# Cross-attention in a two-block fp32 kernel: scores ahead of the value projection, softmax and transposes beside it, output results in pairs

## The chip, the core and the metric

One core of a Trainium2 chip runs the whole program. The metric is the device time of one execution in microseconds; the kernel before took 3685.83 us (median of three runs).

## The reference, cut to what matters

Two transformer-like blocks run one after the other over 256 tokens of width 1024. The first has two layers (l = 0, 1), each a feed-forward network, a mixer, the cross-attention that is changed here, and a second feed-forward network:

```python
def memory_cross_attention(h_n, mem_n, wq, wkv, wo):     # 4 heads of 256
    q = (h_n @ wq).reshape(bsz, seqlen, XA_HEADS, XA_HEAD_DIM)
    mk, mv = jnp.split(mem_n @ wkv, 2, axis=-1)
    ...
    s = jnp.einsum('bshd,bmhd->bhsm', q, mk).astype(jnp.float32) * (XA_HEAD_DIM ** -0.5)
    pr = jax.nn.softmax(s, axis=-1).astype(mv.dtype)
    o = jnp.einsum('bhsm,bmhd->bshd', pr, mv).reshape(bsz, seqlen, D_MODEL)
    return o @ wo

for l in range(DEPTH):                                    # DEPTH = 2
    ...
    h = h + y @ w_mix_out[l]
    h = h + memory_cross_attention(rmsnorm(h, xattn_norm[l]), rmsnorm(mem, mem_norm[l]), xattn_wq[l], xattn_wkv[l], xattn_wo[l])
    h = h + FFN_RES * swiglu_ffn(rmsnorm(h, ffn2_norm[l]), ffn2_w_in[l], ffn2_w_out[l])
```

Everything is fp32. A second block (attention, experts) follows and is the same in both kernels.

## The kernel before, in words

**Weights.** All weights come as one stream of 128x128 blocks, packed into chunks of 32 blocks (2 MB). The SyncE queue loads chunk c into one of three ring slots as soon as the chunk three places earlier is released by TensorE. A product with a weight is made of three fp32r products (`mm3`): high by high, high by low, low by high. So each chunk has to be split before TensorE can use it: a cast into one of two "high" buffers and a subtraction that leaves the low half in the ring slot. In this part of the program VectorE does both (`dve_split`, L389 and L390), and it may not start before TensorE has released the chunk two places earlier, whose high buffer it takes. `act_cast` and `dve_lows` are the same job shared between ScalarE (cast) and VectorE (subtraction). Most products have 96 matmuls of 256 columns to a chunk; those of the value projection have 48 of 512 columns.

**Order.** Each engine's program is a list written in Python order, and an engine runs its list strictly in order. Waits are on counters: `mark(name)` lets an instruction count when it is done, `at(name)` is the value to wait for. VectorE and ScalarE also wait for their own previous instruction. `take` gives out the eight PSUM banks in turn and waits until the bank's last result has been read (`left`).

**Cross-attention of one layer.** Call its first chunk c0. TensorE does, in this order: query projection `xq` (chunks c0, c0+1, eight results of 24 matmuls, with the two norm sums after the first); key projection `xk` (c0+2, c0+3); value projection `xv` (c0+4, c0+5, two halves `n` of two banks each); the attention proper, `pe_attention`; output projection `xout` (c0+6, c0+7). Then the second feed-forward network begins with chunk c0+8: 48 matmuls for its first result, the norm sum, and on. The attention has eight jobs (head h, half of the queries qt). A job is a score product (2 fp32 matmuls), maximum (VectorE), exponential (ScalarE), normalising (VectorE), two transposes on TensorE (`turn`), a copy (ScalarE), the value product (4 fp32 matmuls) and two copies out (VectorE). `Attention.run` staggers them: round i issues the scores of job i+1, the transposes of job i-2 and the values of job i-3. After all eight jobs VectorE makes the high and low halves of the attended values one 128x256 block after the other (L1780, L1781), and `xout` starts when the first is ready.

VectorE's list around this: the split of c0+1; two reciprocals; the normed memory in eight steps of three instructions (L1762, L1764, L1765); four query results; the split of c0+2; four query results; the split of c0+3; and from there each split stands just ahead of the results of the chunk before it. At the end, `xout` result m is added to the stream X (L1785) and two instructions (L525, L526) make the halves that the feed-forward network's products take in the order k = m.

Of the kernel before, what the change touches and what calls it, by code (L numbers as in the profile page):

```python
# [10 lines left out]
ALU = mybir.AluOpType  # L11
# [227 lines left out]
def build(nc, x_t, mem_t, ctx_t, params, consts, na_bias, wexp, xd, yd, out):  # L239
    es = ExitStack()  # L240
    with es:
# [32 lines left out]
        for i, o in enumerate((4096, 5120, 10240, 11264, 17664, 18688, 19712, 20736)):  # L274
            out_parts.append(nc.alloc_sbuf_tensor_at(f"arena_out{i}", [128, 1024], F32R, offset=arena_at + 4 * o))
        psb = [es.enter_context(nc.psum_tensor(f"ps{i}", [128, 512], F32)) for i in range(8)]
# [1427 lines left out]
        XQ, XK, XO, XV = Reg(12288, 2048), Reg(14336, 2048), Reg(16384, 2048), Reg(18432, 2048)  # L1704
        RM = mrow[:, 256:512]

# [3 lines left out]
        def attended_halves(l):  # L1710
            return Halves(("xo", l), lambda k: XO.v(256 * k, 256), lambda k: MN.v(256 * k, 256), as_r)

        def cross(l):
            jobs = []
            for h in range(4):
                for qt in range(2):
                    jobs.append(([XQ.v(256 * (2 * h + j) + 128 * qt, 128) for j in range(2)],
                                 [XK.v(256 * (2 * h + j), 256) for j in range(2)],
                                 [XV.v(1024 * b + 256 * h, 256) for b in range(2)], 256, None,
                                 [XO.v(256 * (2 * h + m) + 128 * qt, 128) for m in range(2)]))  # L1720
            return Attention(("cross", l), jobs, 1.0 / 16, [Reg(20480, 512).v(), Reg(20992, 512).v()],
                             [Reg(21504, 512).v(), Reg(22016, 512).v()],
                             [("left", ("xq", l), 7), ("left", ("xk", l), 6), ("left", ("xk", l), 7), ("left", "xv", l, 1, 1)])

        def pe_xattn(pe, l):
            s = ("xattn", l)
            mh = memory_halves(l)
# [9 lines left out]

            pe_linear(pe, ("xq", l), ("xattn_wq", l), 0, 0, normed(s), range(KT), after=norms)
# [8 lines left out]
            pe_attention(pe, cross(l))  # L1747
            pe_linear(pe, ("xout", l), ("xattn_wo", l), 0, 0, attended_halves(l), range(KT))
            pe.here("pe", "xattn", l)

        def dve_xattn(dve, l):
            s, nxt = ("xattn", l), ("ffn2", l)
            mh, oh = memory_halves(l), attended_halves(l)
            for m in range(KT):
                dve_weights(dve, KT)
                if m == 0:
                    dve_norm(dve, s)
                    dve.wait_ge(*at("mem root", l))
                    dve.next.reciprocal(RM, RM).then_inc(*dve.mark("left", "mem norm", l))
                    for k in range(KT):  # L1760
                        hi, lo = mh.at(k)
                        dve.next.scalar_tensor_tensor(mh.lo(k), MEMr.v(256 * k, 256), par("mem_norm", l, k), RM, ALU.mult,  # L1762
                                                      ALU.mult).then_inc(*dve.mark())
                        dve.next.tensor_copy(hi, mh.lo(k)).then_inc(*dve.mark())  # L1764
                        dve.next.tensor_tensor(lo, mh.lo(k), hi.bitcast(F32), ALU.subtract).then_inc(*dve.mark("half", mh.name, k))  # L1765
# [7 lines left out]
            for n in range(2):  # L1773
                dve_weights(dve, 4 * KT)
                for b in range(2):
                    dve.wait_ge(*at("ps", "xv", l, n, b))
# [1556 lines left out]
```

## Time and profile before

| | |
|---|---|
| median of three runs | 3685.83 us (3681.63 to 3687.85) |
| profiled execution, its own time | 3680.79 us |
| its span in the trace | 3679.0 us |
| TensorE busy | 3409.8 us, 93% |
| VectorE busy | 2854.6 us, 78% |
| ScalarE busy | 1501.6 us, 41% |
| cross-attention, layer 0 and 1 (from the first query product) | about 513 to 642 us and 1350 to 1479 us |

The span is what the rows are measured in. A row of the timeline gives start and duration, then the instruction's group, and in square brackets how long the engine had been idle before it and who released it. TensorE's clock stands in the windows as a share of 2.4 GHz: 1.00 is 2.4 GHz and 0.50 is 1.2 GHz.

### The profile page before, as it was taken

The numbers are of one execution on the slowest core, as the hardware profiler recorded it, in microseconds if no ns is written. First come the engines' busy times: TensorE is split into PE (matmuls) and PEld (weight loads), VectorE is DVE, ScalarE is ACT, GpSimd is POOL, SyncE is SP. The second block draws the span as 40 slices with busy tenths as digits, with TensorE's granted clock in tenths as the row PEclk, the third lists the DMA queues.
The fourth block names the chain that finished last, engine by engine and source line by source line (L and its number), as shares of the span: only waits on it lengthen the run. The fifth ranks groups of instructions, "written<-read, shape, count | busy, mean of one in ns | idle before, by whom it ended". The sixth has DMA issues, their size and how long they took to land.

```text
span 3679.0 us, 53164 instructions
## 1 busy us (share of the span) xinstructions
PE 3409.8 (93%) x21102; PEld 2869.8 (78%) x21102; DVE 2854.6 (78%) x3335; ACT 1501.6 (41%) x2046; POOL 707.4 (19%) x461
## 2 busy tenths in 40 slices
PE   8998999999996999998888999999799789999996
PEld 8996788999994788997555777777687667777775
DVE  8877677888876667876758888888674688888884
ACT  1013121100013121111323888888531358888883
POOL 0000130100000230100001334344101024344430
PEclk9998989999998999999999999999999999999998
DMA  6544243455544243552015999999752169999993
GB/s 238 191 166 190 103 161 118 181 184 184 184 165 183 92 149 123 187 184 92 24 46 187 366 382 374 366 371 376 285 220 103 73 219 346 348 358 344 347 348 134
DMA packets 119853, 799.39 MB, mean 217 GB/s; under 512 B 33824, under 2 KB 35872, under 8 KB 49440
## 3 DMA queue, kind: packets, MB, share of 16 engines
q1 hardware_dynamic: 78480, 735.14, 53.7%
q0 software_dynamic: 39024, 59.61, 4.6%
q8 instruction: 170, 2.79, 0.3%
q10 hardware_dynamic: 2080, 1.05, 0.1%
q14 instruction: 99, 0.81, 0.1%
HBM read 808.77 MB, written 71.83 MB: 239 GB/s over the span
## 4 chain that ended last, share of the span: by engine, by line
PE 54%; DVE 10%; ACT 2%; DMA 1%; issue 1%; POOL 0%; DVEq 0%; SPq 0%; ACTq 0%; POOLq 0%
PE ps L443 50%; PE ps L457 4%; DMA ring<-yd_dram 1%; DVE ring_r L390 1%; DVE ring_r L2650 1%; DVE arena L2094 1%; DVE ring_r L389 0%; ACT arena L1699 0%; DVE mrow L1880 0%; ACT arena_hi L2714 0%; DVE arena_r L2664 0%; DVE arena_r L526 0%; DVE ring L2463 0%; DMA yd_dram<-arena,small 0%; DVE arena L2424 0%
## 5 line engine op out<-in xcount | busy, mean ns | idle before, releaser
L443 PE MATMUL ps<-arena_r,ring_r 128*128 128x256 f32 (+1 forms) x9968 | 1298.1, 290 | 48.5 <-DVE ring_r L390 20.9
L443 PEld LDWEIGHTS ps<-arena_r,ring_r 128*128 128x128 f32 x9968 | 1242.2, 191 | 88.9 <-DVE ring_r L390 21.5
L443 PE MATMUL ps<-ring_r,arena_r 128*128 128x512 f32 (+1 forms) x2906 | 800.5, 391 | 5.5 <-DVE arena_r L1966 5.1
L443 PEld LDWEIGHTS ps<-ring_r,arena_r 128*128 128x128 f32 x2906 | 530.6, 189 | 118.5 <-DVE arena_r L1966 5.5
L443 PE MATMUL ps<-arena_hi,arena_r 128*128 128x512 f32 x1540 | 507.3, 397 | 4.7 <-DVE ring_r L2675 4.7
L390 DVE TENSOR_TENSOR ring_r<-ring,ring_r 128x4096 fp32r<-128x4096 f32 (+2 forms) x108 | 469.5, 4347 | 3.7
L2791 POOL DMA_INDIRECT yd_dram<-arena,small x129 | 227.3, 1762 | 734.2 <-PE ps L457 640.3
L443 PEld LDWEIGHTS ps<-arena_hi,arena_r 128*128 128x128 f32 x1540 | 289.9, 188 | 68.8 <-DVE ring_r L2675 5.1
L389 DVE CAST ring_r<-ring 128x4096 fp32r<-128x4096 f32 (+2 forms) x108 | 268.9, 2490 | 65.0 <-PE ps L443 53.4
L2650 DVE TENSOR_TENSOR ring_r<-ring,ring_r 128x2048 fp32r<-128x2048 f32 x130 | 298.0, 2292 | 22.8 <-ACT ring_r L2714 15.7
L2650 DVE TENSOR_TENSOR ring_r<-ring,arena_hi 128x2048 fp32r<-128x2048 f32 x128 | 293.5, 2293 | 24.2 <-ACT arena_hi L2714 16.8
L2783 POOL DMA_INDIRECT arena<-xd_dram,small x129 | 267.7, 2076 | 150.1 <-DVE arena L2473 60.8
L443 PE MATMUL ps<-ring,arena 128*128 128x512 f32 (+1 forms) x708 | 271.6, 513 | 0.0
L443 PE MATMUL ps<-arena 64*128 64x128 f32 (+5 forms) x1472 | 216.4, 329 | 52.3 <-ACT arena L1699 25.2
L2714 ACT CAST ring_r<-ring 128x2048 fp32r<-128x2048 f32 x130 | 248.8, 1914 | 29.6 <-PE ps L443 18.2
L457 PEld LDWEIGHTS ps<-consts_sb,arena 128*128 128x128 f32 (+1 forms) x1532 | 173.7, 142 | 107.1 <-DVE arena L2669 77.4
L2714 ACT CAST arena_hi<-ring 128x2048 fp32r<-128x2048 f32 x128 | 244.4, 1910 | 11.4 <-ACT arena_hi L2714 0.4
L443 PEld LDWEIGHTS ps<-arena 128*128 128x128 f32 (+1 forms) x1472 | 164.4, 208 | 99.8 <-ACT arena L1699 51.4
L457 PE MATMUL ps<-consts_sb,arena 128*128 128x128 f32 (+1 forms) x1532 | 202.0, 276 | 26.7 <-DVE arena L1175 5.6
L2746 ACT COPY arena<-ps 128x512 f32<-128x512 f32 x258 | 151.2, 586 | 163.6 <-PE ps L443 150.9
L610 ACT ACTIVATE arena<-arena 128x256 f32<-128x256 f32 x88 | 36.8, 418 | 437.4 <-DVE arena L588 437.4
L2664 DVE TENSOR_TENSOR arena_r<-ps,arena_r 128x512 fp32r<-128x512 f32 x258 | 178.5, 692 | 31.1 <-ACT arena_r L2734 3.8
(328 smaller groups left out, 3459.5 us busy)
## 6 DMA issues: line engine op xcount, KB each, us to landing
ring<-wexp_dram SPq DMA_DIRECT2D x387, 1024.0 KB, 8.2
ring<-stream_dram SPq DMA_DIRECT2D x143, 2048.0 KB, 7.8
ring<-yd_dram SPq DMA_DIRECT2D x7, 2048.0 KB, 12.2
arena<-yd_dram SPq DMA_DIRECT2D x5, 2048.0 KB, 9.6
xd_dram<-arena POOLq DMA_DIRECT2D x6, 512.0 KB, 5.9
consts_sb<-consts_dram SPq DMA_DIRECT2D x1, 2242.0 KB, 16.1
arena<-xd_dram,small POOLq DMA_INDIRECT x129, 10.5
yd_dram<-arena,small POOLq DMA_INDIRECT x129, 8.8
```

The costliest lines, as they stand in the source:

```text
L389: dve.next.tensor_copy(chunk_hi(c, a, b), chunk_raw(c, a, b)).then_inc(*dve.mark())
L390: dve.next.tensor_tensor(chunk_lo(c, a, b), chunk_raw(c, a, b), chunk_hi(c, a, b).bitcast(F32), ALU.subtract).then_inc(*dve.mark())
L443: return pe.e.matmul(ps, lhsT=lhsT, rhs=rhs, start=start, stop=stop, skip_group_check=True)
L457: return pe.e.transpose(ps, src, ident[0:n, 0:n])
L610: act.next.activation(g[:, 0:256], g[:, 0:256], ACT.Silu, bias=0.0, scale=1.0).then_inc(*act.mark("silu", s, i))
L2094: dve.next.reciprocal(ARS.v(), ARS.v()).then_inc(*dve.mark("left", "ab norm", i))
L2650: dve.next.tensor_tensor(S.raw(part, i, rings_r), S.raw(part, i), S.hi(part, i).bitcast(F32), ALU.subtract).then_inc(*dve.mark(S.key, "spl ...
L2664: dve.next.tensor_tensor(lo, bank(K, "x", i, g)[:, :], hi.bitcast(F32), ALU.subtract).then_inc(*dve.mark("left", K, "x", i, g))
L2714: act.next.copy(S.hi(part, i), S.raw(part, i)).then_inc(*act.mark(S.key, "high", part, i))
L2746: act.next.copy(YB[i % 2].v(512 * nn, 512), bank(K, "y", i, nn)[:, :]).then_inc(*act.mark("left", K, "y", i, nn))
L2783: pool.e.indirect_dma_start(out=XB[i % 3].v(), out_offset=None, in_=xd, in_offset=bass.IndirectOffsetOnAxis(ap=TOKEN_OF[:, S.b0 + i:S.b0 + ...
L2791: pool.e.indirect_dma_start(out=yd, out_offset=bass.IndirectOffsetOnAxis(ap=PAIR_OF[:, S.b0 + i:S.b0 + i + 1], axis=0), in_=YB[i % 2].v(), ...
```

## The change

In both layers:
- The eight score products come right after `xk`, one in each PSUM bank, before `xv`. VectorE does all eight softmaxes there, ahead of the split of c0+5; the probabilities (`XP`) and their transposes (`XPT`) have a buffer for each job.
- The transposes of job i stand behind step i+3 of the 16 steps of `xv`, the value products of jobs 0 to 3 behind steps 12 to 15. Banks 0 to 3 serve `xv` and `xout`, banks 4 to 7 transposes and values (`take_of`).
- `xout` adds its results up two to a bank ("xout pair"), so that all eight can be open at once: first the products with k = 0, 1 for all m, then the value products of jobs 4 to 7, then k = 2, 3, then m by m k = 4 to 7.
- The attended values' high halves are copied from PSUM by ScalarE (`xo high`) and the low halves made from PSUM by VectorE (`low`), without the copies in between.
- The normed memory's cast goes to ScalarE. The casts of chunks c0+2 and c0+8 go to ScalarE (in quarters), VectorE keeps the subtractions: for c0+2 between the query results 3 and 4, for c0+8 ahead of the `xout` results. The high half of c0+8 has a home of its own (`ffn_parts`).

```diff
+        XP, XPT, XOH = Reg(20480, 2048), Reg(4096, 2048), XK
...
         def pe_xattn(pe, l):
+            cross_at[l] = pe.w.pos // CH
+            hi_home[cross_at[l] + 8] = ffn_parts
+            groups = {0: 0, 4: 0}
+
+            def take_of(first, *name):
+                pe.banks, pe.taken = range(first, first + 4), groups[first]
+                groups[first] += 1
+                return take(pe, *name)
...
+            def turn(i):
+                ps = take_of(4, "xt", l, i)
...
+            def values(i):
+                h = i // 2
+                ps = take_of(4, "xo", l, i)
...
             pe_linear(pe, ("xk", l), ("xattn_wkv", l), 0, 0, mh, range(KT))
+            pe.banks, pe.taken = range(8), 0
+            for i in JOBS:
+                scores(i)
             for n in range(2):
-                pss = [take(pe, "xv", l, n, b) for b in range(2)]
+                pss = [take_of(0, "xv", l, n, b) for b in range(2)]
...
+                    step = KT * n + k
+                    if 3 <= step < 11:
+                        turn(step - 3)
+                    if step >= 12:
+                        values(step - 12)
...
-            pe_attention(pe, cross(l))
-            pe_linear(pe, ("xout", l), ("xattn_wo", l), 0, 0, attended_halves(l), range(KT))
+            out_blocks([(m, k) for k in (0, 1) for m in range(KT)])
+            for i in range(4, 8):
+                values(i)
+            out_blocks([(m, k) for k in (2, 3) for m in range(KT)])
+            out_blocks([(m, k) for m in range(KT) for k in range(4, KT)])
...
         def dve_xattn(dve, l):
+            def normalise(i):
+                mx, sm, nm = softmax_cols(i)
+                dve.wait_ge(*at("left", "xs", l, i))
+                dve.next.reciprocal(sm, sm).then_inc(*dve.mark())
+                dve.next.tensor_scalar(XP.v(256 * i, 256), XP.v(256 * i, 256), sm, None, ALU.mult).then_inc(*dve.mark("xp", l, i))
...
             for m in range(KT):
+                if m == KT // 2:
+                    dve_lows(dve, c0 + 2, ((0, n_),), 1024)
                 dve_weights(dve, KT)
...
-            for n in range(2):
-                dve_weights(dve, 4 * KT)
...
-            dve_attention(dve, cross(l))
-            for k in range(KT):
-                dve.next.tensor_copy(oh.at(k)[0], oh.lo(k)).then_inc(*dve.mark())
...
+            for i in range(10):
+                if i < 8:
+                    largest(i)
+                if i >= 2:
+                    normalise(i - 2)
+            dve_weights(dve, 4 * KT)
+            values_out(0)
+            dve_weights(dve, 4 * KT)
+            for i in range(4):
+                low(i)
+            values_out(1)
+            dve_weights(dve, 4 * KT)
+            for i in range(4, 8):
+                low(i)
+            dve_lows(dve, c0 + 8, QUARTERS, 1024)
+            dve_weights(dve, 4 * KT)
             for m in range(KT):
-                dve_weights(dve, KT)
-                dve.wait_ge(*at("ps", ("xout", l), m))
...
+                dve.wait_ge(*at("ps", "xout pair", l, m // 2))
...
         def act_xattn(act, l):
+            for k in range(KT):
+                act.wait_ge(*at("mem normed", l, k))
+                act.next.copy(mh.at(k)[0], mh.lo(k)).then_inc(*act.mark("mem high", l, k))
+            act_cast(act, c0 + 2, QUARTERS, "released", c0)
...
-            act_attention(act, cross(l))
+            for i in JOBS:
...
+                              v3(bank("xo", l, i)[:, 0:256], 128)).then_inc(*act.mark("xo high", l, i))
+            act_cast(act, c0 + 8, QUARTERS, "ps", "xv", l, 1, 1)
```

On TensorE, before, the end of `xv` (banks 3 and 4) and the start of the attention (`arena`, fp32; L457 is a transpose) read:

```order
L443 MATMUL ps4<-ring_r_49,arena_r_50 128x512 x3
L443 MATMUL ps3<-ring_r_49,arena_r_50 128x512 x3
L443 MATMUL ps4<-ring_r_49,arena_r_50 128x512 x3
L443 MATMUL ps5<-arena 128x256 [waits dve_done,act_done]
L443 MATMUL ps5<-arena 128x256
L443 MATMUL ps6<-arena 128x256 x2
L443 MATMUL ps7<-arena 128x256 x2
L443 MATMUL ps0<-arena 128x256 x2
L457 MATMUL ps1<-consts_sb,arena 128x128 [waits dve_done]
L457 MATMUL ps1<-consts_sb,arena 128x128
L443 MATMUL ps2<-arena 128x256 x2
L443 MATMUL ps3<-arena 128x128 [waits act_done]
```

In the change (L445 is the same helper line), TensorE from the last key product (bank 0) to the start of `xv`:

```order
L445 MATMUL ps0<-arena_r_50,ring_r_49 128x256 x24
L445 MATMUL ps0<-arena 128x256 [waits dve_done,act_done]
L445 MATMUL ps0<-arena 128x256
L445 MATMUL ps1<-arena 128x256 x2
L445 MATMUL ps2<-arena 128x256 [waits dve_done]
L445 MATMUL ps2<-arena 128x256
L445 MATMUL ps3<-arena 128x256 x2
```

and its last steps of `xv` with the value products of jobs 2 and 3 (banks 6, 7), then the first `xout` pairs:

```order
L445 MATMUL ps2<-ring_r_49,arena_r_50 128x512 x3
L445 MATMUL ps3<-ring_r_49,arena_r_50 128x512 x3
L445 MATMUL ps6<-arena 128x128 [waits act_done]
L445 MATMUL ps6<-arena 128x128 x3
L445 MATMUL ps2<-ring_r_49,arena_r_50 128x512 x3
L445 MATMUL ps3<-ring_r_49,arena_r_50 128x512 x3
L445 MATMUL ps7<-arena 128x128 [waits act_done]
L445 MATMUL ps7<-arena 128x128 x3
L445 MATMUL ps0<-arena_r_50,ring_r_49 128x256 [waits dve_done]
L445 MATMUL ps0<-arena_r_50,ring_r_49 128x256 x5
```

The scores moved ahead of `xv` and wait for the last key result's copy, whose bank 0 is the first that they take; the value products moved between steps of `xv`, and `xout` follows without the eight-job block ahead of it.

On VectorE, before, from the last two key results to the end of `xv`'s results (`ring`: splits, L1777: value results), and then the first softmax:

```order
L1772 COPY arena<-ps 128x256 [waits dve_done,pe_done] x2
L389 CAST ring_r<-ring 128x4096 [waits dve_done,pe_done,chunk_loaded1]
L390 TENSOR_TENSOR ring_r<-ring,ring_r 128x4096 [waits dve_done]
L1777 COPY arena<-ps 128x512 [waits dve_done,pe_done] x2
L389 CAST ring_r<-ring 128x4096 [waits dve_done,chunk_loaded2]
L390 TENSOR_TENSOR ring_r<-ring,ring_r 128x4096 [waits dve_done]
L1777 COPY arena<-ps 128x512 [waits dve_done,pe_done] x2
L1657 TENSOR_REDUCE small<-ps 128x1 [waits pe_done]
```

In the change, the end of the eight softmaxes, then the splits of c0+5, c0+6 and c0+7 (L391, L392) among the value results (L1836) and the attended values (L1828):

```order
L1823 TENSOR_SCALAR arena<-arena,small 128x256 [waits dve_done]
L391 CAST ring_r<-ring 128x4096 [waits dve_done,chunk_loaded1]
L392 TENSOR_TENSOR ring_r<-ring,ring_r 128x4096 [waits dve_done]
L1836 COPY arena<-ps 128x512 [waits dve_done,pe_done] x2
L391 CAST ring_r<-ring 128x4096 [waits dve_done,chunk_loaded2]
L392 TENSOR_TENSOR ring_r<-ring,ring_r 128x4096 [waits dve_done]
L1828 TENSOR_TENSOR arena_r<-ps,arena_r 128x2x128 [waits dve_done,act_done] x4
L1836 COPY arena<-ps 128x512 [waits dve_done,pe_done] x2
L391 CAST ring_r<-ring 128x4096 [waits dve_done,pe_done,chunk_loaded0]
L392 TENSOR_TENSOR ring_r<-ring,ring_r 128x4096 [waits dve_done]
L1828 TENSOR_TENSOR arena_r<-ps,arena_r 128x2x128 [waits dve_done,act_done] x4
```

The split of c0+5 moved from directly behind the last key result to behind 32 softmax instructions.

## Rows read from the trace of the kernel before

**Rows 1.** Windows of layer 0, cut where TensorE's stages begin; busy us.
```profile
544.83:571.29 26.46, 23.94 (x192) 23.94 (x193) 19.31 (x13) 1.12 (x3) 0.00 (x0) 0.94 0.44 160
571.40:593.96 22.56, 22.56 (x98) 17.90 (x96) 15.48 (x7) 1.66 (x2) 0.00 (x0) 1.00 0.51 187
593.96:616.34 22.38, 17.52 (x114) 14.89 (x113) 14.36 (x53) 7.49 (x24) 0.00 (x0) 1.00 0.26 95
616.34:642.20 25.86, 25.45 (x193) 24.55 (x194) 24.28 (x32) 2.04 (x5) 0.00 (x0) 0.94 0.22 82
642.20:655.11 12.91, 11.10 (x65) 10.10 (x64) 10.99 (x12) 2.58 (x5) 0.00 (x0) 0.87 0.45 164
```

Columns of Rows 1: stretch and length, then busy time of TensorE's matmuls, its weight loads, VectorE, ScalarE and GpSimd (instructions), TensorE's clock, DMA share, GB/s.

**Rows 2.** Timeline, TensorE: queries into keys (layer 0), the same in layer 1, its end.
```profile
524.52 20.31 PE L443 MATMUL ps<-arena_r,ring_r 128*128 128x256 f32 x168
547.35 12.90 PE L443 MATMUL ps<-arena_r,ring_r 128*128 128x256 f32 x95 [2.52 <-DVE ring_r L390]
...
1384.45 24.12 PE L443 MATMUL ps<-arena_r,ring_r 128*128 128x256 f32 x192 [2.52 <-DVE ring_r L390]
...
1490.62 9.66 PE L443 MATMUL ps<-arena_r,ring_r 128*128 128x256 f32 x79
```

**Rows 3.** Timeline, ScalarE, layer 0: the copy of the last key result.
```profile
571.60 0.37 ACT L1796 COPY arena<-ps 128x256 f32<-128x256 f32 x1 [5.23 <-PE ps L443]
```

**Rows 4.** Timeline, TensorE inside the attention: scores with values, transposes, scores with values.
```profile
601.05 1.92 PE L443 MATMUL ps<-arena 128*128 128x256 f32 x12
602.81 0.38 PE L457 MATMUL ps<-consts_sb,mrow 128*128 128x128 f32 x2
603.03 2.07 PE L443 MATMUL ps<-arena 128*128 128x256 f32 x12
```

**Rows 5.** Timeline, TensorE, start of the second feed-forward network: products, norm sum, products.
```profile
645.64 0.62 PE L443 MATMUL ps<-arena_r,ring_r 128*128 128x256 f32 x3 [0.82 <-DVE arena_r L526]
647.07 4.94 PE L443 MATMUL ps<-arena_r,ring_r 128*128 128x256 f32 x27 [0.82 <-DVE arena_r L526]
651.85 3.62 PE L443 MATMUL ps<-arena,consts_sb 128*128 128x256 f32 x16
655.11 1.05 PE L443 MATMUL ps<-arena_r,ring_r 128*128 128x256 f32 x6
```

**Rows 6.** Timeline, VectorE: normed memory, query results, the split of c0+2.
```profile
527.89 0.48 DVE L1762 SCALAR_TENSOR_TENSOR arena<-arena,params_sb,mrow 128x256 f32<-128x256 f32 x1
528.41 0.29 DVE L1764 CAST arena_r<-arena 128x256 fp32r<-128x256 f32 x1
528.74 0.42 DVE L1765 TENSOR_TENSOR arena_r<-arena,arena_r 128x256 fp32r<-128x256 f32 x1
...
538.42 2.01 DVE L1767 TENSOR_TENSOR arena<-ps,mrow 128x256 f32<-128x256 f32 x4
540.54 2.29 DVE L389 CAST ring_r<-ring 128x4096 fp32r<-128x4096 f32 x1
542.87 4.43 DVE L390 TENSOR_TENSOR ring_r<-ring,ring_r 128x4096 fp32r<-128x4096 f32 x1
```

**Rows 7.** Timeline, ScalarE in the second block: a chunk cast in quarters.
```profile
2698.03 4.28 ACT L402 CAST ring_r<-ring 128x1024 fp32r<-128x1024 f32 x4
```

**Rows 8.** Timeline, VectorE: maximum and scaling of one job, normalising of another.
```profile
604.20 0.42 DVE L1657 TENSOR_REDUCE small<-ps 128x1 f32<-128x256 f32 x1
604.65 0.15 DVE L1658 TENSOR_SCALAR small<-small 128x1 f32<-128x1 f32 x1
...
605.85 0.16 DVE L1648 RECIPROCAL small<-small 128x1 f32<-128x1 f32 x1
606.05 0.35 DVE L1649 TENSOR_SCALAR arena<-arena,small 128x256 f32<-128x256 f32 x1
```

**Rows 9.** DMA issues, 500 to 660 us: KB each, median us to landing.
```profile
ring<-stream_dram SPq DMA_DIRECT2D x9, 2048.0 KB, 8.1
```

**Rows 10.** The page's costliest groups: transposes; busy us, mean ns of one, idle before.
```profile
L457 PE MATMUL ps<-consts_sb,arena 128*128 128x128 f32 (+1 forms) x1532 | 202.0, 276 | 26.7 <-DVE arena L1175 5.6
```

More of the change, by code:

```diff
@@ L275, in build @@
             out_parts.append(nc.alloc_sbuf_tensor_at(f"arena_out{i}", [128, 1024], F32R, offset=arena_at + 4 * o))
+        ffn_parts = [nc.alloc_sbuf_tensor_at(f"arena_ffn{i}", [128, 1024], F32R, offset=arena_at + 4 * o) for i, o in enumerate((8192, 9216))]
+        ffn_parts += out_parts[2:4]
         psb = [es.enter_context(nc.psum_tensor(f"ps{i}", [128, 512], F32)) for i in range(8)]
@@ L1710, in attended_halves, with attended, softmax_cols @@
         def attended_halves(l):
[L1711 to L1723, printed above, removed]
+            return Halves(("xo", l), lambda k: XO.v(256 * k, 256), lambda k: XOH.v(256 * k, 256), as_r)
+        def attended(reg, i):
+            return v3(reg[:, 512 * (i // 2):512 * (i // 2) + 512], 256)[:, :, col(i % 2)]
+        def softmax_cols(i):
+            return [small[:, 200 + 4 * i + j:201 + 4 * i + j] for j in range(3)]
         def pe_xattn(pe, l):
             s = ("xattn", l)
-            mh = memory_halves(l)
+            mh, oh = memory_halves(l), attended_halves(l)
+            cross_at[l] = pe.w.pos // CH
[5 more added lines that the diff above has]
+                return take(pe, *name)
             def norms(m):
@@ L1746, in pe_xattn, with out_blocks @@
                             *(("ps", "xv", l, n, b) if k == KT - 1 else ()), last=b == 1)
-            pe_attention(pe, cross(l))
-            pe_linear(pe, ("xout", l), ("xattn_wo", l), 0, 0, attended_halves(l), range(KT))
+                    step = KT * n + k
[3 more added lines that the diff above has]
+                        values(step - 12)
+            pairs = {}
+            def out_blocks(order):
+                for m, k in order:
+                    wb = blocks(pe, ("xattn_wo", l), 128 * k, 128 * m)
+                    if m % 2 == 0 and k == 0:
+                        pairs[m // 2] = take_of(0, "xout pair", l, m // 2)
+                    pe.wait_ge(*at("half", oh.name, k))
+                    mm3(pe, pairs[m // 2][:, col(m % 2, 256)], wb, oh.at(k), k == 0 and m % 2 == 0, k == KT - 1,
+                        *(("ps", "xout pair", l, m // 2) if k == KT - 1 and m % 2 else ()))
+            out_blocks([(m, k) for k in (0, 1) for m in range(KT)])
[3 more added lines that the diff above has]
+            out_blocks([(m, k) for m in range(KT) for k in range(4, KT)])
+            pe.banks = range(8)
             pe.here("pe", "xattn", l)
@@ L1796, in act_xattn @@
                 act.next.copy(XK.v(256 * m, 256), bank(("xk", l), m)[:, 0:256]).then_inc(*act.mark("left", ("xk", l), m))
-            act_attention(act, cross(l))
+            for i in JOBS:
+                mx, sm, nm = softmax_cols(i)
+                act.wait_ge(*at("xmax", l, i))
+                act.next.activation(XP.v(256 * i, 256), bank("xs", l, i)[:, 0:256], ACT.Exp, bias=nm, scale=1.0 / 16,
+                                    accum_out=sm).then_inc(*act.mark("left", "xs", l, i))
+            for i in JOBS:
+                act.wait_ge(*at("ps", "xt", l, i))
+                act.next.copy(XPT.v(256 * i, 256), bank("xt", l, i)[:, 0:256]).then_inc(*act.mark("left", "xt", l, i))
+            for i in JOBS:
+                act.wait_ge(*at("ps", "xo", l, i))
+                act.next.copy(attended(arena_r[:, XOH.base:XOH.base + 2048], i),
+                              v3(bank("xo", l, i)[:, 0:256], 128)).then_inc(*act.mark("xo high", l, i))
+            act_cast(act, c0 + 8, QUARTERS, "ps", "xv", l, 1, 1)
             for m in range(KT):
```

61 lines of the change are left out of this document (49 added, 12 removed).

## The prediction

> **What bounds the kernel now.** I read the page first (TensorE is busy for 93% of the span), then TensorE's timeline through the cross-attention of both layers, then windows cut where its stages begin, and last the timelines of VectorE and ScalarE for what releases it. TensorE's order is one long chain, so what counts is how much longer each stage takes than its products need.
>
> The needs first. A key result, 48 matmuls at two results, takes 0.37 + 5.23 = 5.60 us by the copies' rhythm [rows 3], so 192 matmuls take 22.4 us, and 48 take 5.6. The value projection takes 22.56 us with TensorE never idle [rows 1]. One score product and one value product together take 602.81 - 601.05 = 1.76 us, a job's two transposes 603.03 - 602.81 = 0.22 us [rows 4]; eight jobs need 14.1 + 1.8 = 15.9 us. The norm sum takes 655.11 - 651.85 = 3.26 us [rows 5]. From the end of the queries (544.83 us) to 655.11 us the products need 22.4 + 22.56 + 15.9 + 22.4 + 5.6 + 3.26 = 92.1 us.
>
> The stretch lasts 110.28 us, so 18.2 us are lost in layer 0, in four places [rows 1]:
> - Keys: 26.46 against 22.4, 4.1 lost. TensorE waits 2.52 us for the split of c0+2 [rows 2], and the window's mean clock is 0.94; the remaining 1.5 us is work done at half clock after the wait.
> - Attention: 22.38 against 15.9, 6.5 lost in round trips over VectorE and ScalarE.
> - Output: 25.86 against 22.4, 3.5 lost: `xout` begins while VectorE still makes halves, at a mean clock of 0.94.
> - Feed-forward start: 12.91 against 5.6 + 3.26, 4.0 lost: two waits of 0.82 us are shown for the last stream halves [rows 5], because results 4 to 7 stand behind a split, and the clock is 0.87 [rows 1].
>
> Layer 1 repeats this (the same 2.52 us wait, queries ending at 1384.45 - 2.52 = 1381.93) but is through at 1490.62 [rows 2]: 108.69 us, 16.6 lost. The clock does not drop at its end.
>
> **The change, part by part.** No product is added or removed on TensorE; the gain is the lost time less what is lost afresh. VectorE and ScalarE I walk through in their new order.
>
> Memory norm and c0+2. The memory's loop on VectorE starts at 527.89. A first product takes 0.52 us to the next start, a low 0.42 + 0.04; with the cast on ScalarE a step costs 0.98 instead of about 1.30, eight end at 536.2, four query results (2.01) at 538.2 [rows 6]. ScalarE has its last memory cast behind it at about 535.7 (the nearest row is a copy of 0.37 us, [rows 3]). It may then cast c0+2, since c0 is released after 72 of the 168 matmuls, at 524.52 + 72 x 0.121 = 533.2 [rows 2]. Four quarters take 4.28 us [rows 7]: 540.0. VectorE's subtraction takes 4.43 [rows 6]: 544.5. TensorE asks at 544.83. The 2.52 us wait goes, with 0.3 us to spare, and with it the half clock. If the casts come 2 us late, 1.7 us of wait returns, at worst with its 1.5 us of clock.
>
> What is late next: c0+3's split starts when four query results are out (546.6), takes 6.81 (540.54 to 547.35, [rows 2, 6]) and ends at 553.4; it is needed at 544.8 + 11.2 = 556.0.
>
> Scores and softmax. I now count from the end of the keys as t = 0. The first score takes bank 0, which holds the last key result, so it waits for ScalarE's copy: that starts 0.31 us after the keys end (571.29 to 571.60) and lasts 0.37 [rows 1, 3], with the signal 0.7 us. This is new idle time. Scores then run to 0.7 + 8 x 0.88 = 7.7 (0.88 is half of 1.76). On VectorE a job costs 0.42 + 0.15 + 0.16 + 0.35 [rows 8] and four gaps of 0.04, together 1.24 us; the first three maxima follow the scores (to 4.0), and the five maxima of 0.64 and eight normalisings of 0.60 left end at 12.0. Only then comes the split of c0+5, to 18.9. TensorE asks for it after half of the value projection and five jobs' transposes, at 7.7 + 11.3 + 1.1 = 20.1. It is hidden by 1.2 us; beyond that each microsecond costs one, and a wait like that of the keys brings its 1.5 us of clock.
>
> Value projection. It ends, with eight transposes and four value products (0.88), at 7.7 + 22.56 + 1.8 + 3.5 = 35.5. The split of c0+6 is ready at 20.1 + 1.5 + 6.9 = 28.5, the halves of jobs 0 and 1 well before. Behind it stand the halves of jobs 2 and 3, `xv` results and c0+7's split: 36.4 + 1.5 + 6.8 = 44.7, needed at 35.5 + 5.6 + 3.5 + 5.6 = 50.2.
>
> c0+8. Its slot is free at 34.7, a chunk lands 8.1 us after its issue [rows 9], 42.8. ScalarE reaches its casts after the last value copy, at 45.1, and ends at 49.4; VectorE's four quarters follow to about 50.5. The first `xout` pair is ready at 53.0, so nothing waits for it. A landing over 2.5 us later would hold the results behind the subtractions.
>
> Output. The last pair is ready at T = 50.2 + 11.2 = 61.4. VectorE handles one result in 647.07 - 645.64 = 1.43 us [rows 5], 2.86 a pair against 2.8 for TensorE to make one, so it has the last half ready at T + 3.1; TensorE asks for it at T + 7 x 0.35 = T + 2.45. Pairing costs 0.7 us here, in place of 4.0.
>
> Insertions. The transposes and values between `xv` steps bring 16 changes of product and wait per layer. The trace has none next to fp32r products of `xv`; in the attention the ends meet without a gap. Bounds: nothing, and one transpose slot of 0.11 us each, 1.8 us a layer. I take the middle, 0.9.
>
> Here the Trainium skill speaks against the move. Its page "TensorE: Matmul & The Clock Gate", section "Part 4: PE-mode transpose", gives about 275 ns to a transpose in a kernel. By that alone 16 transposes would take 4.4 us a layer. The profile's group agrees as a duration, 276 ns mean [rows 10], but durations overlap: two follow one another in 0.22 us [rows 4], so the sum above uses 0.11 each.
>
> **Sum.** Fresh losses are 0.7 + 0.7 + 0.9 = 2.3 us a layer. Layer 0 gains 18.2 - 2.3 = 15.9, layer 1 gains 16.6 - 2.3 = 14.3, together 30.2 us. I take 30: the span goes from 3679.0 to 3649, the profiled execution from 3680.8 to 3651. The median of before is 3685.83, 5 us above its profiled execution, and the forecast goes with the median: 3655.8 us. The feed-forward network behind runs on the same chunk rhythm, so the gain should reach the end.
>
> **The rivals.**
> - Transposes pay their full duration inside `xv`: 16 x 0.276 = 4.4 us instead of 1.8, 2.6 us more a layer. For: the 276 ns [rows 10]. Against: the spacing of 0.11 us [rows 4]. Gain 30 - 5.2, time 3661.
> - The softmax keeps its old pace. An old round lasted 603.03 - 601.05 = 1.98 us [rows 4]; eight at that pace from t = 1.7 end at 17.5, the split of c0+5 at 24.3, and TensorE waits 4.2 us plus 1.5 for the clock. For: VectorE needs the scores and ScalarE's exponentials between its steps. Against: the old pace was that of the round trip with TensorE, which is now gone. It costs 5.7 a layer: 3667.
> - c0+2 stays late, as the order on ScalarE has no slack of size: 3.2 us a layer, 3662.
> - The stream cannot deliver. The chunks are now used up in some 12 us each. Against: in the value projection the stream moved 187 GB/s while TensorE was never idle [rows 1], and a landing takes 8.1 us. If it did hold TensorE to the old mean, nothing would change: 3686.
> - Slower than before: the split of c0+5 behind 32 softmax instructions. The same mechanism as the second, from 3.2 us per job on: then the split ends at 33.7, TensorE waits 13.6 us and the clock takes 1.5, which eats the mean gain of a layer, 15.1. At 4 us a job the split ends at 40.5, the loss is 20.4 + 1.5 us a layer, and the time is 3699. Against: the rows add up to 1.24 us a job.
>
> **How the numbers follow.** The forecast with all splits hidden gets 0.72; transposes at full length 0.06, old softmax pace 0.08, c0+2 late 0.09, the stream 0.03, slower 0.02. The low end is all 34.8 us of lost time without any fresh loss, 3651, and 3 us for the spread between runs (3681.63 to 3687.85): 3648. The high end takes in the partial cases up to 3668. Within 0.2% (7.4 us) is what a measurement here cannot tell from no change. Faster 0.95, same 0.03, slower 0.02.
>
> **What would show it.** Right: the timeline of TensorE has no wait for a ring subtraction (L410, L392) at the start of the keys or in `xv`; windows through the whole cross-attention show clock 1.00; a wait of 0.7 us ahead of the scores and of about 0.7 for the last stream half; the stretch from the queries' end to the end of the feed-forward norm sum lasts 94 to 95 us in both layers. Wrong: a VectorE wait at c0+2 or in the middle of `xv`, a clock of 0.5 behind it, `xv` with its insertions far over 28 us, or a gain in the cross-attention that later stages give back.

## The result, and the profile after

The changed kernel took 3646.84 us (median of four, 3641.68 to 3652.22), the kernel before beside it 3683.73 us (3676.8 to 3687.85): a ratio of 0.99 with a 95% interval of 0.9887 to 0.9914. The forecast was 3655.8 us with a range of 3648 to 3668, so the result lies 1.2 us below the range. The profiled execution took 3648.08 us, its span 3646.3 us, 32.7 us less than before.

The windows of layer 0 after the change (columns as in [rows 1]; queries, keys, scores, value projection with its insertions, output projection, feed-forward start). One cut differs: [rows 1] cuts the keys at the end of the last query product, these windows at its start, 0.28 us earlier; the other cuts are alike.

```profile
521.94:541.80 19.86, 19.86 (x169) 19.83 (x168) 16.50 (x23) 7.94 (x13) 0.00 (x0) 1.00 0.29 107
541.80:564.60 22.80, 22.80 (x195) 22.68 (x193) 16.99 (x13) 1.12 (x3) 0.00 (x0) 1.00 0.51 185
564.60:572.16 7.56, 7.10 (x35) 6.09 (x34) 4.36 (x16) 4.45 (x12) 0.00 (x0) 1.00 0.77 277
572.16:600.21 28.05, 28.05 (x147) 23.11 (x145) 20.51 (x26) 5.83 (x18) 0.00 (x0) 1.00 0.21 76
600.21:626.95 26.74, 26.43 (x227) 26.20 (x226) 22.59 (x31) 8.59 (x15) 0.00 (x0) 1.00 0.43 158
626.95:636.48 9.53, 9.18 (x66) 8.59 (x65) 9.11 (x9) 2.12 (x3) 0.00 (x0) 1.00 0.60 222
```

The clock is 1.00 in every stage, where [rows 1] had 0.94, 0.94 and 0.87. The keys take 22.52 us (22.80 less the 0.28) instead of 26.46. The 22.38 us of the attention are gone: 7.56 us of scores stand alone, the value projection grew from 22.56 to 28.05 us by the transposes of eight jobs and the value products of four, and the value products of the other four are in the 26.74 us of the output stage. From the end of the last query product to behind the feed-forward norm sum it is 94.4 us in layer 0 (542.08 to 636.49) and 94.5 in layer 1; 94 to 95 was forecast.

The waits that are left, from TensorE's timeline after the change (layer 0, and the first of layer 1):

```profile
565.34 7.17 PE L445 MATMUL ps<-arena 128*128 128x256 f32 x32 [0.46 <-ACT arena L1897]
602.16 4.57 PE L445 MATMUL ps<-arena_r,ring_r 128*128 128x256 f32 x36 [0.31 <-DVE arena L1836]
629.94 0.51 PE L445 MATMUL ps<-arena_r,arena_ffn 128*128 128x256 f32 x2 [0.35 <-DVE arena_r L528]
...
1365.39 22.67 PE L445 MATMUL ps<-arena_r,ring_r 128*128 128x256 f32 x192 [0.45 <-DVE ring_r L410]
```

A bracket counts idle time from the end of the product before, and a product's row lasts 0.28 us where the next one can start 0.12 us behind it. So a wait costs about 0.2 us more than its bracket says.

The first is the wait for bank 0 and the copy of the last key result, the third the wait for the last stream half; both were forecast. The second was not: the third output pair takes bank 2, and the value projection's second half in it is read (L1836) only behind job 3's low half. The fourth is c0+2 in layer 1, whose 0.3 us of slack was a 0.45 us wait there. In layer 0 it had no slack either: the subtraction ends at 541.95 us and the first key product starts at 542.00, 0.08 us late, and 0.26 us late in the four other traces of the change.

VectorE after the change, around c0+5's split (L391, L392):

```profile
568.23 0.42 DVE L1816 TENSOR_REDUCE small<-ps 128x1 f32<-128x256 f32 x1 [0.25 <-PE ps L445]
569.61 0.43 DVE L1816 TENSOR_REDUCE small<-ps 128x1 f32<-128x256 f32 x1
570.98 0.42 DVE L1816 TENSOR_REDUCE small<-ps 128x1 f32<-128x256 f32 x1
577.96 2.29 DVE L391 CAST ring_r<-ring 128x4096 fp32r<-128x4096 f32 x1
580.29 4.43 DVE L392 TENSOR_TENSOR ring_r<-ring,ring_r 128x4096 fp32r<-128x4096 f32 x1
```

A softmax job takes 1.37 us, not 1.24, and the split ends at 584.72. TensorE's next rows show that it was just late:

```profile
582.80 0.38 PE L459 MATMUL ps<-consts_sb,arena 128*128 128x128 f32 x2
582.94 1.64 PE L445 MATMUL ps<-ring_r,arena_r 128*128 128x512 f32 x6
584.41 0.38 PE L459 MATMUL ps<-consts_sb,arena 128*128 128x128 f32 x2
584.77 1.66 PE L445 MATMUL ps<-ring_r,arena_r 128*128 128x512 f32 x6
```

Behind transposes the next product starts after 0.14 us, but here after 0.36: 0.2 us of wait, where 1.2 us of slack was forecast.

### The profile page after: what moved, and what is told of

Its sections match the earlier page's. It is cut to its first block, busy times and chain, and to the rows that moved or that the text cites. A ratio compares the mean times of both kernels' runs of the same rounds, so it can differ in the third digit from the quotient of the medians.

```text
span 3646.3 us, 53228 instructions
## 1 busy us (share of the span) xinstructions
PE 3396.7 (93%) x21102; PEld 2859.7 (78%) x21102; DVE 2827.4 (78%) x3273; ACT 1531.6 (42%) x2094; POOL 710.2 (19%) x461
## 4 chain that ended last, share of the span: by engine, by line
PE 56%; DVE 9%; ACT 2%; DMA 1%; issue 1%; POOL 0%; DVEq 0%; SPq 0%; ACTq 0%; POOLq 0%
PE ps L445 52%; PE ps L459 4%; DMA ring<-yd_dram 1%; DVE ring_r L2763 1%; DVE arena L2207 1%; DVE ring_r L392 0%; ACT arena L1701 0%; DVE mrow L1993 0%; ACT arena_hi L2827 0%; DVE ring_r L410 0%; ACT ring_r L404 0%; DVE ring L1226 0%; DVE ring L2576 0%; DVE arena_r L2777 0%; DVE ring_r L391 0%
## 5 line engine op out<-in xcount | busy, mean ns | idle before, releaser
L445 PE MATMUL ps<-arena_r,ring_r 128*128 128x256 f32 (+1 forms) x9840 | 1281.0, 289 | 35.2 <-DVE ring_r L392 15.5
L445 PEld LDWEIGHTS ps<-arena_r,ring_r 128*128 128x128 f32 x9840 | 1222.5, 190 | 72.1 <-DVE ring_r L392 15.7
L445 PE MATMUL ps<-ring_r,arena_r 128*128 128x512 f32 (+1 forms) x2906 | 806.5, 392 | 5.6 <-DVE arena_r L2079 5.2
L445 PEld LDWEIGHTS ps<-ring_r,arena_r 128*128 128x128 f32 x2906 | 529.0, 189 | 117.7 <-DVE arena_r L2079 5.6
L445 PE MATMUL ps<-arena_hi,arena_r 128*128 128x512 f32 x1540 | 507.7, 397 | 4.7 <-DVE ring_r L2788 4.7
L392 DVE TENSOR_TENSOR ring_r<-ring,ring_r 128x4096 fp32r<-128x4096 f32 (+2 forms) x104 | 451.8, 4344 | 3.6
L445 PEld LDWEIGHTS ps<-arena_hi,arena_r 128*128 128x128 f32 x1540 | 290.4, 189 | 69.3 <-DVE ring_r L2788 5.1
L391 DVE CAST ring_r<-ring 128x4096 fp32r<-128x4096 f32 (+2 forms) x104 | 259.8, 2498 | 58.0 <-PE ps L445 46.5
L445 PE MATMUL ps<-ring,arena 128*128 128x512 f32 (+1 forms) x708 | 270.2, 510 | 0.0
L459 PEld LDWEIGHTS ps<-consts_sb,arena 128*128 128x128 f32 x1540 | 175.0, 142 | 108.6 <-DVE arena L2782 76.2
L445 PE MATMUL ps<-arena 64*128 64x128 f32 (+5 forms) x1472 | 212.2, 328 | 44.1 <-ACT arena L1701 20.8
L445 PEld LDWEIGHTS ps<-arena 128*128 128x128 f32 (+1 forms) x1472 | 163.9, 209 | 88.3 <-ACT arena L1701 43.2
L459 PE MATMUL ps<-consts_sb,arena 128*128 128x128 f32 x1540 | 203.2, 276 | 26.9 <-DVE arena L1288 5.6
L2777 DVE TENSOR_TENSOR arena_r<-ps,arena_r 128x512 fp32r<-128x512 f32 x258 | 178.4, 692 | 30.8 <-ACT arena_r L2847 3.5
## 6 DMA issues: line engine op xcount, KB each, us to landing
consts_sb<-consts_dram SPq DMA_DIRECT2D x1, 2242.0 KB, 15.9
```

What stands on the lines that cost most here:

```text
L391: dve.next.tensor_copy(chunk_hi(c, a, b), chunk_raw(c, a, b)).then_inc(*dve.mark())
L392: dve.next.tensor_tensor(chunk_lo(c, a, b), chunk_raw(c, a, b), chunk_hi(c, a, b).bitcast(F32), ALU.subtract).then_inc(*dve.mark())
L445: return pe.e.matmul(ps, lhsT=lhsT, rhs=rhs, start=start, stop=stop, skip_group_check=True)
L459: return pe.e.transpose(ps, src, ident[0:n, 0:n])
L2777: dve.next.tensor_tensor(lo, bank(K, "x", i, g)[:, :], hi.bitcast(F32), ALU.subtract).then_inc(*dve.mark("left", K, "x", i, g))
```

## The experiments

In each trace I read where three same products start: the first query product behind the norm sums, the first product behind the feed-forward norm sum, and the same in layer 1. "Layer 0" and "layer 1" are these two stretches; "outside" is the rest between TensorE's first and last product. All in us:

| kernel | layer 0 | layer 1 | outside | timed median |
|---|---|---|---|---|
| before (5 traces) | 130.5 to 130.8 | 128.9 to 129.3 | 3387.1 to 3393.1 | see below |
| changed (5 traces) | 114.3 to 114.5 | 114.4 to 114.7 | 3383.2 to 3396.4 | see below |
| p_c2 | 126.5 | 126.9 | 3393.6 | 3677.4 |
| u_c2 | 118.8 | 119.0 | 3386.4 | 3655.7 |
| u_xout | 119.7 | 119.8 | 3386.2 | 3660.3 |
| k_slack | 117.9 | 119.2 | 3395.2 | 3661.9 |
| u_inter | 118.4 | 120.5 | 3391.2 | 3656.4 |
| u_inter2 | 115.8 | 116.3 | 3387.0 | 3649.8 |
| best | 113.0 | 112.3 | 3392.1 | 3647.7 |

The two stretches repeat within 0.4 us; outside, the same kernel scatters by up to 13 us. So parts are judged by the stretches. Their sums are 259.7 before and 228.9 after, a gain of 30.8 us.

**The part on c0+2, alone and undone.** p_c2 is the kernel before with this part (the memory's cast and the cast of c0+2 on ScalarE) and no more; u_c2 is the changed kernel without it.

```diff
+                if m == KT // 2:
+                    dve_lows(dve, c0 + 2, ((0, n_),), 1024)
...
+            for k in range(KT):
+                act.wait_ge(*at("mem normed", l, k))
+                act.next.copy(mh.at(k)[0], mh.lo(k)).then_inc(*act.mark("mem high", l, k))
+            act_cast(act, c0 + 2, QUARTERS, "released", c0)
```

> The kernel before with one part of the change alone: the memory's cast and the cast of c0+2 on ScalarE, the subtraction of c0+2 between query results 3 and 4. Theory: the 2.52 us wait at the start of the keys shrinks to 0 to 0.5 us and the half clock behind it goes, 3.6 to 4.1 us a layer, 7 to 8 us in all. Rival: the wait only moves to the next split (c0+3 or c0+4), and less than 3 us is gained in all.

> The changed kernel with that part undone: memory cast and c0+2's split on VectorE as before. Theory: the 2.5 us wait and 1.5 us of half clock return in each layer, 7 to 8 us more than the changed kernel. Rival: if the parts depend on each other (VectorE then is also late for c0+5, which had no slack left), more than 10 us.

Alone it gave 6.3 us in the stretches (4.1 in layer 0, 2.2 in layer 1) and a ratio of 0.998 (0.9972 to 0.9989). Undone it cost 8.9 us, 4.5 and 4.4. In p_c2 layer 0 has no wait in the keys; layer 1 shows:

```profile
1377.71 22.88 PE L443 MATMUL ps<-arena_r,ring_r 128*128 128x256 f32 x192 [0.43 <-DVE ring_r L408]
```

and u_c2 in layer 0 the old wait, with 192 products in 24.21 us:

```profile
545.80 24.21 PE L445 MATMUL ps<-arena_r,ring_r 128*128 128x256 f32 x192 [2.53 <-DVE ring_r L392]
```

So 6.3 us is under the 7 to 8 expected and 8.9 us above it; three of the four layers are near the 4.1 us of the prediction. Layer 1 alone gave less, and the trace shows why: its wait and the half clock behind it went, but TensorE's clock now stood at 1.2 GHz from 1476.31 us on, at the start of the feed-forward network, where none of the five traces of before has that in layer 1. The same 27 products, p_c2 and then before:

```profile
1476.10 4.97 PE L443 MATMUL ps<-arena_r,ring_r 128*128 128x256 f32 x27 [0.81 <-DVE arena_r L526]
```

```profile
1484.09 3.42 PE L443 MATMUL ps<-arena_r,ring_r 128*128 128x256 f32 x27 [0.81 <-DVE arena_r L526]
```

That took back 1.55 us. Why the clock fell there was not tested.

**The order of the output products undone.**

```diff
-            out_blocks([(m, k) for k in (0, 1) for m in range(KT)])
             for i in range(4, 8):
                 values(i)
-            out_blocks([(m, k) for k in (2, 3) for m in range(KT)])
-            out_blocks([(m, k) for m in range(KT) for k in range(4, KT)])
+            out_blocks([(m, k) for m in range(KT) for k in range(KT)])
```

> The changed kernel with the order of the output products undone: the value products of jobs 4 to 7 directly behind the value projection, then the output results one after the other, k from 0 to 7, still in pairs of a bank. Theory: the halves of jobs 4 to 7 stand behind c0+7's split on VectorE, so TensorE waits about 5 us at k = 4 of the first result and then runs 1.5 us longer at half clock: 10 to 14 us more than the changed kernel in all. Rival: the order of the output products is worth little, under 4 us, since the value products themselves give VectorE the time.

It cost 10.6 us in the stretches (ratio to before 0.9937, 0.9923 to 0.9951). The size is the theory's (10 to 14 us), the place only in part:

```profile
603.09 0.46 PE L445 MATMUL ps<-arena 128*128 128x128 f32 x2 [1.81 <-DVE arena L1834]
603.79 5.24 PE L445 MATMUL ps<-arena 128*128 128x128 f32 x30 [0.24 <-DVE arena L1834]
611.71 21.63 PE L445 MATMUL ps<-arena_r,ring_r 128*128 128x256 f32 x180 [1.27 <-DVE arena_r L1826]
```

The wait for the low halves is 1.27 us, not 5. Ahead of it stands 1.81 us for the value projection's second half, which jobs 4 to 7 multiply by, and the 30 records behind take 5.24 us, since the clock fell to 1.2 GHz at 604.53 us; 32 such records take 3.73 us in the changed kernel. In the changed order 48 output products stand ahead of these value products, and only 0.31 us of wait is left. Layer 1 shows the same rows.

**Slack of c0+5's split.** Every maximum twice:

```diff
-                dve.next.tensor_reduce(mx, bank("xs", l, i)[:, 0:256], AX.X, ALU.max).then_inc(*dve.mark())
+                for _ in range(2):
+                    dve.next.tensor_reduce(mx, bank("xs", l, i)[:, 0:256], AX.X, ALU.max).then_inc(*dve.mark())
```

> The changed kernel with every maximum of the softmax computed twice, 8 x 0.46 = 3.7 us more on VectorE ahead of c0+5's split. Theory: that split has no slack left (it came 0.2 us late in the trace after), so TensorE waits 3.9 us more at the middle of the value projection and may run 1.5 us longer at half clock: 7 to 11 us more in all. Rival: the split has the 1.2 us of slack that the prediction gave it, 5 us or less.

It cost 8.2 us in the stretches, 3.6 and 4.6 (ratio to before 0.994, 0.9927 to 0.9953). In layer 0 and in layer 1:

```profile
589.76 1.65 PE L445 MATMUL ps<-ring_r,arena_r 128*128 128x512 f32 x6 [3.36 <-DVE ring_r L392]
...
1417.12 2.65 PE L445 MATMUL ps<-ring_r,arena_r 128*128 128x512 f32 x6 [3.18 <-DVE ring_r L392]
```

Counted from the start of the last key product, the split ends 3.37 us later than in the changed kernel (23.49 against 20.12), and the product that needs it starts 3.37 us later: the slack is zero. In layer 1 the clock was at 1.2 GHz behind the wait (six products in 2.65 us instead of 1.65), in layer 0 it was not.

**Transposes and values as a block.** u_inter puts all transposes and values behind the value projection; u_inter2 also reads the second half of its results first.

```diff
-                    if 3 <= step < 11:
-                        turn(step - 3)
-                    if step >= 12:
-                        values(step - 12)
+            for i in JOBS:
+                turn(i)
+            for i in JOBS:
+                values(i)
...
-            for i in range(4, 8):
-                values(i)
...
+            values_out(1)
             for i in range(4):
                 low(i)
-            values_out(1)
```

> The changed kernel with transposes and value products not between the value projection's steps: all eight jobs' transposes and then all eight value products stand behind it, the output products keep the new order. Theory: what counts is that the softmax is done early and that the output order gives VectorE time; in one block the transposes are paced by ScalarE's copies, about 1.3 us a layer, so 2 to 4 us more in all. Rival: the place between the weight products is what hides the attention; then about 4 us a layer come back, over 7 us in all.

> As the run with transposes and values in one block behind the value projection, but VectorE reads the second half of the value projection's results ahead of the low halves of jobs 0 to 3, which job 4's value product had waited 1.8 us for. Theory: of the 9.9 us that the block cost in the two stretches, 3.5 to 4.5 come back; what stays is the late split of c0+5 (1.1 us a layer, it loses the cover of the transposes) and the transposes paced by ScalarE's copies, 5 to 7 us in all. Rival: the wait moves to the next low half and under 2 us come back.

u_inter cost 9.9 us in the stretches (ratio to before 0.9928, 0.9917 to 0.994), so my theory fell (2 to 4 us). Its rows in layer 0:

```profile
587.45 11.43 PE L445 MATMUL ps<-ring_r,arena_r 128*128 128x512 f32 x48 [1.15 <-DVE ring_r L392]
...
607.04 0.46 PE L445 MATMUL ps<-arena 128*128 128x128 f32 x2 [1.80 <-DVE arena L1833]
```

The second wait is again that for the late value results (L1833); in layer 1, 1.2 GHz followed it, and the 30 records behind took 5.24 us against 3.62 in layer 0. With that mended, u_inter2 costs 3.1 us (ratio 0.9913, 0.9898 to 0.9929): 6.8 came back, more than the 3.5 to 4.5 expected. So the place of the transposes and values is worth 1.6 us a layer, of which the wait for c0+5's split, which loses their cover, is 1.14 us in layer 0 and 0.96 in layer 1. The rest of u_inter's loss came from one pair of copies in the wrong place of VectorE's list, through its wait and what followed.

**Three waits removed.**

```diff
-            pe.banks, pe.taken = range(8), 0
+            pe.banks, pe.taken = (1, 0, 2, 3, 4, 5, 6, 7), 0
...
-                    dve_lows(dve, c0 + 2, ((0, n_),), 1024)
+                    dve_lows(dve, c0 + 2, QUARTERS, 1024)
...
-            for i in range(4):
+            for i in range(3):
                 low(i)
             values_out(1)
+            low(3)
```

> The changed kernel with three waits of the trace after taken away: the first score takes bank 1 and the second bank 0, so that it needn't wait for the last key result (0.46 us a layer); the value results are read ahead of job 3's low half, so that the third pair's bank is free (0.31 us a layer); the subtraction of c0+2 in quarters behind the casts (0.45 us in layer 1). Theory: 1.5 to 2.5 us less than the changed kernel in the trace's two stretches, too little for the timed medians to tell apart. Rival: the first wait only moves to the first maximum or to c0+5's split, and under 1 us is gained.

The stretches shrink by 3.6 us to 225.3, more than the 1.5 to 2.5 expected, and of the waits only the last stream half's is listed (0.35 us). The brackets had told too little: from the last key product to the first value product it is 6.84 us instead of 7.56 in layer 0, 0.72 us for a wait listed with 0.46. The timed median, 3647.7 us (ratio to before 0.9903, 0.989 to 0.9916), can't be told from the changed kernel's 3649.14 and 3647.2.

No run takes the part on c0+8 away alone, nor only the early softmax. Their shares are read from the windows and not shown by a run: the feed-forward start went from 12.91 to 9.53 us.

**The same kernels again.**

> The changed kernel once more, unaltered. Theory: the cross-attention gives 15.8 us in layer 0 and 14.2 us in layer 1, 30.0 us in all, and what the first comparison showed beyond it (32.7 us between the profiled spans, 36.9 us between the medians) is scatter between executions in stretches that the change does not touch. Then five rounds should give 28 to 34 us less than before, and a new trace should again have about 94.5 us in each layer from the queries' end to the end of the norm sum, with the rest of the span moved by a few us either way. Rival: the code behind or ahead of the cross-attention really runs some 6 us shorter because it starts at another moment; then the gain is again 36 to 38 us.

> The kernel before, unaltered, for a second trace. Theory (scatter outside the cross-attention): its cross-attention stretches again last 130 and 129 us from the first query product behind the norm sums to the end of the feed-forward norm sum, within 0.5 us, while the mixers and the second block differ from the first trace by 1 to 4 us each, and the ratio is 1 within 0.2%. Rival (the code outside is really slower before than after): all three other stretches are longer than in every trace of the changed kernel.

The changed kernel took 3649.14 us (ratio 0.9906, 0.9893 to 0.992), 34.8 us less than before: above the theory's 28 to 34, below the rival's 36 to 38. The kernel before took 3684.29 us (ratio 1.0003), with stretches of 130.6 and 128.9 us, as expected.

> The kernel before again, for a third trace. Open: the timed medians differ by 35 us, the cross-attention by 30.6 us in the traces, and both traces of before are of executions 3 to 7 us under its median. Theory (chance): the stretches outside the cross-attention add up to 3387 to 3396 us in both kernels. Rival (the code outside is slower before): here they add up to 3394 us or more, in the changed kernel to 3390 or less.

> The changed kernel again, for a third trace; theory: outside the cross-attention 3387 to 3396 us, the same range as before; rival: 3390 us or less.

> The kernel before, a fourth trace. Theory (chance): outside the cross-attention 3387 to 3396 us; rival: 3394 us or more.

> The changed kernel, a fourth trace. Theory (chance): outside the cross-attention 3387 to 3396 us; rival: 3390 us or less.

Outside, the two traces of before have 3393.1 and 3392.3 us, the two of the change 3383.2 and 3396.4. The range 3387 to 3396 holds for before, and the rival's 3394 is not reached; of the change one is far under the range, as the rival has it, and one just above it, against the rival. These traces decide nothing.

> The changed kernel once more, timed in five rounds. The traces of four executions each give 30.7 us in the cross-attention and 32.0 us between the mean spans; the timed medians give 35. Theory (the traces happened to be of quick executions before): over five new rounds the difference comes nearer to 31, within 29 to 34. Rival (some 4 us outside the cross-attention are real and only hidden in the traces' scatter): again 34 to 37.

> The kernel before, timed in five rounds beside the changed one, for the same question. Theory: a median of 3680 to 3684; rival: 3683 or more. A fifth trace: cross-attention stretches of 130.6 and 129.1 us within 0.3 us.

The changed kernel took 3647.2 us (ratio 0.9901, 0.9886 to 0.9917), 35.1 us less than before, in the rival's range; the kernel before 3681.97 us (1.0001), in the theory's. All executions together: 79 of before with a mean of 3683.3 us, 15 of the change with 3648.2 us, a difference of 35.2 us; with standard deviations of 3.8 and 3.9 us its standard error is 1.1 us. That is more than the 30.8 us of the stretches. So the rival holds: chance alone does not explain it. The five traces each don't show it well, since their executions of before lie 2.5 us under the mean.

The other kernels can be asked the same. The six variants of the changed kernel (33 executions) lie on average 3.5 us further below 3683.3 us than their stretches say (standard error 0.8), from -0.3 for k_slack to 5.8 for u_c2; for the twelve executions of p_c2 it is 0.2 us. So the gain outside goes with the large change, not with the part on c0+2.

One part outside has a place. The second feed-forward network of layer 1, the same code, runs at two paces. Windows of 100 us inside it, before and after:

```profile
1500.00:1600.00 100.00, 100.00 (x852) 100.00 (x851) 89.29 (x72) 7.53 (x18) 12.50 (x17) 1.00 0.50 185
```

```profile
1470.00:1570.00 100.00, 100.00 (x859) 100.00 (x859) 90.25 (x72) 7.54 (x18) 13.28 (x18) 1.00 0.51 186
```

TensorE never idles and its clock is 1.00 in both, yet 852 or 859 products fit in. From the first product of this network to the 1501st it is 176.86 us in all five traces of before and in p_c2, and 175.24 us in all five traces of the change and in its six variants: 1.6 us. It is not fixed by the code alone: the same stretch of layer 0 takes 175.19 us in four traces of before and 176.86 in the fifth. What sets the pace was not found.

## Why the prediction was right and wrong

- **Keys and c0+2.** Right in place and size: 26.46 us became 22.52 in layer 0, and undoing it cost 4.5 us a layer. The 0.3 us of slack was mis-sized: TensorE can take the first key product about 0.16 us before the row of the last query product ends, and in layer 1 one step of the memory's loop waits 0.46 us for ScalarE. The lateness is 0.1 to 0.3 us in layer 0 and 0.6 in layer 1.
- **Scores.** Right: in the prediction's own count, from the start of the last key product to the first score, the wait for bank 0 is 565.34 - 564.60 = 0.74 us, 0.7 forecast. The 0.46 us of the row is its bracket.
- **Softmax and c0+5.** The split is hidden but for 0.2 us; the 1.2 us of slack was mis-sized: the gaps between dependent VectorE instructions are up to 0.11 us and not 0.04, so a job takes 1.37 us and not 1.24. k_slack shows what hung on it.
- **Insertions.** Forecast at half a slot each, 0.9 us a layer, and not paid. In the value stage 22.56 + 8 x 0.22 + 4 x 0.88 = 27.84 us explain all but 0.2 of the 28.05 us, and 0.2 is the split's wait. A pair of transposes with the six products behind it takes 1.61 us (582.80 to 584.41), six products alone take 22.56 / 16 = 1.41, so the pair costs 0.20 us of TensorE's time, though its row lasts 0.38. The Trainium skill ("TensorE: Matmul & The Clock Gate", section "Part 4: PE-mode transpose") gives about 275 ns for one; the trace shows that this duration is not what one costs in a stream.
- **Output and feed-forward start.** The feed-forward start took 9.53 us, which is 0.67 more than the 8.86 it needs (0.7 forecast; the row's bracket says 0.35), without half clock. The output stage took 26.74 us where 22.4 + 3.5 = 25.9 was forecast: the wait for bank 2 (0.31 us in the bracket, 0.5 between starts) was missed.
- **Sum.** 15.9 and 14.3 us were forecast for the layers; by the means of five traces the stretches give 16.3 and 14.5. Both are right, but the fit is partly luck: 0.9 us for insertions that cost nothing stand against 0.8 us missed in the output stage and 0.2 us at c0+5's split.
- **What failed** is the step from the sum to the time. The prediction put the gain outside the cross-attention at nothing ("the gain should reach the end") and took its low end from that: "The low end is all 34.8 us of lost time without any fresh loss, 3651, and 3 us for the spread between runs". The executions show 35.2 - 30.8 = 4.4 us of gain outside, with a standard error of 1.1; 1.6 us of it are in the feed-forward network of layer 1, and the cause of this and of the rest stays open. The 9.0 us between 3655.8 and 3646.84 are made up so: 2.5 us because the median of three before, 3685.83, was above the mean of 79, 3683.3; 0.8 us more in the stretches than 30; 1.6 us in that feed-forward network; 1.3 us because the four executions lay under the mean of 15, 3648.2; and 2.8 us left, outside and without a place. The reference alone decides the miss: with 3683.3 us in place of 3685.83 the same working has its low end at 3645.5, under the measured time.

## What to carry to other kernels

When engines pass small results back and forth while a large preparation waits its turn, count each place in the preparing engine's list: two copies of 1.5 us together behind the wrong instructions cost more here (6.8 us) than moving all transposes and values out of the covering stream (3.1 us). Price a wait from start to start: the bracket of a row left out 0.2 us and more each time. What a stage's stretch gains can be forecast from rows within 1 us; what the whole program gains can't, when executions scatter by 13 us outside the change, so a range needs that scatter, not the spread of three runs. Check which PSUM bank a moved result takes first: its last reader becomes a wait.

## What the runs showed of the hardware

- The scatter outside goes with TensorE's clock, in the traces of the change more closely than in those of before. From the first feed-forward product of layer 0 to the queries of layer 1 two traces of the changed kernel differ by 6.7 us:

```profile
636.49:1345.00 708.51, 658.68 (x5385) 0.94 0.45 166
```

```profile
637.34:1339.15 701.81, 650.99 (x5384) 0.96 0.45 168
```

(Columns: stretch, length, TensorE's busy time, clock, DMA share, GB/s.) The clock stood at 1.2 GHz for 85.3 and 61.4 us of them. In the three others 68.3, 78.5 and 81.9 us go with lengths of 705.6, 705.3 and 707.5 us; in two traces of before the same 71.7 us go with 706.1 and 703.3. Which causes which was not tested.
- A wait is not always followed by the half clock. c0+2's 2.53 us were, with 192 products in 24.21 us; the 3.36 us of k_slack in layer 0 were not, its layer had no time at 1.2 GHz at all, while the 3.18 us of the same wait in layer 1 were. The 1.80 us wait of u_inter was followed by it in layer 1 and not in layer 0.
- A stream of the same products with TensorE always busy at full clock has two paces, 0.1167 and 0.1178 us from start to start. Both occur in one trace: in the changed kernel's the keys of layer 0 run at 0.1178 and those of layer 1 at 0.1167.
- Two fp32 transposes follow one another in 0.11 us though each has a duration of 0.27, and a pair in a stream of 512-column products costs 0.20 us.
